# Reading eight retention states over four column groups, with five gate projections moved among them

## The chip, the cores and the metric

One core of a Trainium2 chip runs the whole decoder step as one launch. The metric is device time in microseconds (us) of one launch. Engines are named as in the profile: PE (matrix products) with its weight loads PEld, DVE (vector), ACT (activation), POOL (GpSimd, which here also issues the state transfers) and SP (which issues the weight transfers). Each engine works through its own list in order and meets the others at semaphores.

## The reference, cut to what matters

The step has 256 prompt tokens and a sample group of 8 sequences with one new token each (264 columns in all), a model width of 1024 and everything in float32. The change touches the retention branch of the sample group and the order around it:

```
q, k: 4 heads of 256 (rotary);  v: 4 heads of 512;  g: 2048;  gates g_a, g_b, g_c: 1024 each
for each of 8 sequences b, each of 4 heads h, with s = state_ret[b, h]  (256 x 512):
    s_new = gamma_h * s + k[b,h] (outer) v[b,h]          -> ret_s, an output of 16 MB
    o[b,h] = q[b,h] @ s_new                              (512 numbers)
o = o / sqrt(mean(o*o) + eps) per head
b_out  = (silu(g) * o) @ w_branch_ret
merged = sigmoid(g_a)*a_out + sigmoid(g_b)*b_out + sigmoid(g_c)*c_out ;  x = x + merged @ w_out
then RMSNorm, a mixture of 32 experts over all tokens, residual, final RMSNorm
```

## The kernel before

A Python list, made by `tensor_order()`, holds every task, and each engine walks the same list and does its own part of each task. So a task's place in the list is its place in the queue of PE, ACT and DVE alike; nothing is planned by cost. A projection (`ga`, `lru_out`, `gc`, `mem_out`, `gb`, `g`, ...; lines 988 and 997 in `project`) makes one 128-row tile of output from eight 128x128 weight blocks; each float32 product shows as two instructions in the profile, so it has 16. Projections take turns in PSUM banks 0 to 3, other tasks in banks 4 to 6, and the state reads keep bank 7. Weights come in chunks of two projections (1 MB) into a ring of five places, in list order; SP issues a chunk once the chunk five before it has been used.

**The state stretch.** The 8 x 4 states are handled as 16 steps s of two heads (1 MB each) in three buffers. For each step:

- POOL loads the state (line 895), once that buffer's earlier state is stored and read. It also brings the step's row of v to one partition (line 901) and, when that small transfer has landed, broadcasts it to all partitions (line 905).
- ACT waits for the load and multiplies the state by gamma (task `sd`, two instructions of 128x1024).
- DVE adds the outer product in four instructions of 128x512 (task `sd`, line 1654).
- PE reads the new state against a one-column-per-sequence arrangement of q called `QM` (task `so`, line 1193), and POOL stores it (line 920).

POOL's order is: wait for step s to be updated, store s, bring and broadcast v of s+2, load state s+2. The PE part of `so` for heads 2hp and 2hp+1 writes each head to its own group of 32 PSUM partitions (of 8 used rows):

```
for i in range(2):
    for h2 in range(2):
        h = 2 * hp + h2
        mm = pe.matmul(psum[32 * h:32 * h + NS, 7, :], QM[:, 2 * h + i, b, :], st[:, s % 3, 2 * h2 + i, :], ...)
```

An older task of the same kind, `sc` (line 1132, the sample group's cross-attention), writes four heads to four groups in turn, two products of 256 columns for each head, so 16 instructions in the profile.

**What is woven around it.** The 32 projections `ga`, `lru_out`, `gc`, `mem_out`, woven with the prompt's retention (`att`, four `o`, two `S` per head; lines 1159/1162, 1172/1173, 1181), are the main list, and the 32 items `sd`/`so` are spread evenly over it. In the list, `sd4` stands just before `ga7`, and `att1`, `so3`, `lru_out0`, `o10` follow. `o10` (line 1172) needs DVE's masked copy of `att1` (line 1644), and DVE has `sd4` ahead of it.

**After it.** The eight `gb` projections are woven with `soT` (line 1201: four transposes that bring the 8 tokens' o back to columns), `oq` (squares, ACT, which at the first one waits until all states are stored), and `on` (PE column sums at line 1007, ACT root, DVE lines 1667 and 1669). Then come 16 `g`, 8 `ret_out`, 8 `x2`, the router and the loop over expert pairs.

Of the kernel before, what the change touches and what calls it, by code (L numbers as in the profile page):

```python
# [33 lines left out]
P = 128  # L34
D = 1024
# [27 lines left out]
def shape_constants():  # L63

    f = np.float32
    half = DK // 2
    inv = np.power(f(ROPE_BASE), -np.linspace(0.0, 1.0, half, dtype=f)).astype(f)
    pos = np.concatenate([np.arange(TP), np.full(NS, PAST_LEN)]).astype(f)
    ang = (inv[:, None] * pos[None, :]).astype(f)
    log_g = np.log1p(-(2.0 ** (-5.0 - np.arange(HEADS))))  # L70
    p = np.arange(P)
    mask = np.zeros((P, HEADS, 384))
    for h in range(HEADS):
        n = np.arange(TP)
        mask[:, h, :TP] = np.where(n[None] >= p[:, None], np.exp(np.maximum(n[None] - p[:, None], 0) * log_g[h]), 0)
        mask[:, h, TP:] = mask[:, h, :P]
    kdec = np.zeros((P, 2, HEADS))
    for mt in range(2):
        kdec[:, mt, :] = np.exp((TP - 1 - (mt * P + p))[:, None] * log_g[None])
    valid = np.ones((P, TT))  # L80
    valid[T - 2 * P:, 2] = 0
    parts = {
        "cos": np.cos(ang), "sin": np.sin(ang), "dmask": mask.reshape(P, -1),
        "ident": np.eye(P), "kdec": kdec.reshape(P, -1), "before": (p[:, None] < p[None, :]).astype(f), "valid": valid,
        "slot": np.tile(np.arange(SLOTS), (P, 1)), "count32": np.tile(np.arange(EXPERTS), (P, 1)),
        "count8": np.tile(np.arange(OVER), (P, 1)),
    }
    at, cols, off = {}, [], 0
    for name, a in parts.items():
        at[name] = (off, off + a.shape[1])  # L90
        off += a.shape[1]
        cols.append(a.astype(f))
    return np.ascontiguousarray(np.concatenate(cols, axis=1)), at
# [8 lines left out]

BUFFERS = {
    "rope": (NROPE, "load", "v"),
    "dmask": (NMASK, "load", "gc"),
    "const": (NCONST - NROPE - NMASK, "load", "end"),
    "ones": (P, "load", "end"),
    "chan": (12 * KT, "load", "end"),
# [34 lines left out]
    "uyT": (KT * T, "uy", "ga"),  # L143
    "lru_st": (KT * 16, "ux", "end"),
    "conv_st": (KT * 16, "ux", "end"),
    "qT": (KT * T, "q", "gc"),
    "kT": (KT * T, "k", "gc"),
    "rtmp": (HEADS * 2 * T, "k", "v"),
    "vT": (VT * T, "v", "rows"),
    "v_rows": (2 * HEADS * DV, "rows", "gc"),  # L150
    "k_rows": (2 * D, "v", "gc"),
    "vs_rows": (HEADS * DV, "rows", "gc"),
    "v_row0": (D, "rows", "gc"),
    "vb": (2 * D, "rows", "gc"),
    "st": (3 * 4 * DV, "rows", "gc"),
    "p32": (TP, "k", "k"),
    "PM": (512, "k", "v"),
    "cs": (TP, "k", "rows"),
    "QM": (KT * 64, "k", "gc"),
    "attT": (384, "rows", "gc"),  # L160
    "oT": (VT * T, "ga", "ret"),
    "S_st": (2 * DV, "ga", "gb"),
    "os": (DV, "ga", "gb"),
# [74 lines left out]
def weave(main, side):  # L238

    out, n = [], 0  # L240
    for i, m in enumerate(main):
        out.append(m)
        while n * len(main) < (i + 1) * len(side):
            out.append(side[n])
            n += 1
    return out


def tensor_order():

    t = lambda kind, n: [(kind, i) for i in range(n)]
    heads = range(HEADS)
    lg = [[("lg", h, 0), ("lg", h, 1)] for h in heads]
    pv = [[("pT", h), ("pv", h, 0), ("pv", h, 1)] for h in heads]  # L270
    attn = lg[0] + lg[1] + pv[0] + lg[2] + pv[1] + lg[3] + pv[2] + pv[3]
    gates = [x for n in range(KT) for x in (("r", n), ("i", n))]
    kl = t("kl", NS)
    cache = [("sl",), ("spT",)] + t("sc", NS)
    krows = [("kr", m, q) for m in range(2) for q in range(2)]
    v = t("v", VT)
    vrows = t("vs", 4) + [("vr", m, q) for q in range(4) for m in range(2)]
    ret = []
    for h in heads:
        ret += [("att", h)] + [("o", h, j) for j in range(4)] + [("S", h, i) for i in range(2)]  # L280

    so = [("sd", 0)]
    for s in range(2 * NS):
        so += ([("sd", s + 1)] if s + 1 < 2 * NS else []) + [("so", s)]
    branches = t("ga", 8) + t("lru_out", 8) + t("gc", 8) + t("mem_out", 8)
    onorm = [("soT",), ("oq", 0), ("oq", 1), ("on", 0), ("oq", 2), ("on", 1), ("oq", 3), ("on", 2), ("on", 3)]
    return (

        [("mem_sq",)] + t("mk", 8)[:2] + [("xq",)] + t("mk", 8)[2:4] + [("x_sq",), ("lam",)] + t("mk", 8)[4:]
        + weave(t("mv", 8), t("mkT", 4)) + t("mq", 8) + t("mqs", 2)  # L290

        + weave(t("ux", 8), weave(attn[:11], kl[:2])) + [("conv",)] + weave(t("uy", 8), weave(attn[11:], kl[2:5]))

        + weave(t("q", 8), weave(gates, kl[5:])) + weave(t("k", 8)[:3], cache[:2]) + [("rot_q",)]
        + weave(t("k", 8)[3:], cache[2:5]) + [("rot_k",), ("lru",)]

        + weave(v[:6], cache[5:]) + [("lru_root",), ("gelu",)] + weave(v[6:12], krows) + [("gelu_tanh",)] + v[12:]
        + [("scT",)] + vrows + ret[:1]

        + weave(weave(branches, ret[1:]), so)  # L300

        + weave(t("gb", 8), onorm) + t("g", 16) + t("ret_out", 8) + t("x2", 8) + [("x2_sq",)]
    )


# [27 lines left out]
def build_program(nc, dram, outs, const_at):  # L333
# [55 lines left out]
    with ExitStack() as ctx:  # L389
# [76 lines left out]
        PM = buf("PM").rearrange("p (m h b c) -> p m h b c", m=2, h=HEADS, b=NS)  # L466
        PMd = place_of["PM"]
        cs = buf("cs")
        QM = buf("QM").rearrange("p (k b c) -> p k b c", k=KT, b=NS)
        QMd = place_of["QM"]  # L470
        attT = buf("attT")
        oT = tiles(buf("oT"), VT)
# [38 lines left out]
        def diagonal(at, n):  # L511

            return arena[:, at:at + 64 * n].rearrange("p (k x) -> p k x", x=64)[:, :, 0:64:9]

        psum = ctx.enter_context(nc.psum_tensor("psum", [P, 8, 512], F32))

# [70 lines left out]
        def ps(task):  # L587
            return psum[:, where[task][0], :]
# [372 lines left out]
        def _(pe):  # L961
# [56 lines left out]
            for task in order:  # L1018
# [156 lines left out]
                elif kind == "S":  # L1175
                    _, h, i = task
                    if i == 0:
                        read(pe, ("kr", 1, 1))
                    begin(task)
                    for m in range(2):  # L1180
                        mm = pe.matmul(ps(task)[:, 0:DV], k_rows[:, m, (2 * h + i) * P:(2 * h + i + 1) * P],  # L1181
                                       v_rows[:, m, h * DV:(h + 1) * DV], start=m == 0, stop=m == 1)
                    end(task, mm)
                elif kind == "so":
                    s = task[1]
                    b, hp = n_state(s)
                    if s == 0:
                        pe.wait_ge(bank7_zero, 2)
                    pe.wait_ge(st_updated, s + 1)
                    for i in range(2):  # L1190
                        for h2 in range(2):
                            h = 2 * hp + h2
                            mm = pe.matmul(psum[32 * h:32 * h + NS, 7, :], QM[:, 2 * h + i, b, :],  # L1193
                                           st[:, s % 3, 2 * h2 + i, :],
                                           start=b == 0 and i == 0, stop=b == NS - 1 and i == 1)
                    mm.then_inc(st_read, 1)
                elif kind == "soT":
                    read(pe, ("so", 0))
                    begin(task)
                    for j in range(4):  # L1200
                        mm = pe.transpose(ps(task)[:, j * P:(j + 1) * P], os_[:, j * P:(j + 1) * P], ident)
                    end(task, mm)
                elif kind == "on":
                    pe.wait_ge(squares, 5 + task[1])
                    column_sums(task, sq2[:, task[1] % 2], 4, T)
                elif kind == "x2_sq":
                    residual_squares(KT - 2)
                    end(task, residual_squares(KT - 1))
                else:
                    raise AssertionError(kind)  # L1210
# [266 lines left out]
        def _(dve):  # L1477
# [17 lines left out]
            for task in order:  # L1495
# [100 lines left out]
                elif kind in ("rot_q", "rot_k"):  # L1596
# [3 lines left out]
                    cos, sin = (bc(k_(n).unsqueeze(1), (P, HEADS, T)) for n in ("cos", "sin"))  # L1600
                    read(dve, last["q" if kind == "rot_q" else "k"])

                    full(dve, ("i", KT - 1))
                    v(V.tensor_tensor(t1, x2_, sin, ALU.mult))
                    v(V.tensor_tensor(t2, x1, sin, ALU.mult))
                    v(V.tensor_tensor(x1, x1, cos, ALU.mult))
# [3 lines left out]
                    if kind == "rot_q":  # L1610
                        v(V.memset(QM, 0.0))

                        v(V.tensor_copy(diagonal(QMd, KT), qT[:, :, TP:T]))
                elif kind == "sl":

                    full(dve, ("i", KT - 1))
                    v(V.memset(buf("PM"), 0.0))
                    v(V.memset(psum[:, 7, :], 0.0), bank7_zero)
                    full(dve, task)
# [37 lines left out]
                elif kind == "soT":  # L1657
                    full(dve, task)
                    for h in range(HEADS):
                        did(V.tensor_copy(oT[:, 4 * h:4 * h + 4, TP:T],  # L1660
                                          ps(task).rearrange("p (j c) -> p j c", j=4)[:, :, 32 * h:32 * h + NS]),
                            free_of(task) if h == HEADS - 1 else None)
                elif kind == "on":
                    h = task[1]
# [256 lines left out]
```

## Time and profile before

| | us |
|---|---|
| device time, median of 3 runs | 1262.12 (1260.25 to 1269.47) |
| span of the profiled execution | 1255.6 |
| own device time of the profiled execution | not listed beside its span; the three timed runs are 4.7 to 13.9 above it, their median 6.5 |
| PE busy | 1185.2 (94%) |
| DVE / ACT / POOL busy | 385.5 / 237.3 / 100.3 |
| first to last state read (PE, line 1193) | 333.1 to 500.8 |
| end of the `gb` and norm stage, first `g` | 540.5 |

The span runs from the first to the last instruction of the profiled execution. Times inside the trace count from the start of the span.

### The profile page before, as it was taken

Reading aid. Unit: us, or ns where it says so; the run is one execution under the profiler, and the core shown is the slowest. Engines: PE = TensorE matmul, PEld = TensorE weight load, DVE = VectorE, ACT = ScalarE, POOL = GpSimd, SP = SyncE. Lnnn points to the kernel's source line nnn. Section 1 sums busy time; section 2 is a strip of 40 time slices with the busy share of each in tenths; the row PEclk is TensorE's granted clock in tenths of the full one; section 3 lists DMA queues with packets and bytes.
Section 4 is the critical chain, followed back from the end, with each engine's and each line's share of the span. In section 5 each row is a group of like instructions: output and inputs, shape, how many; then the busy total and the mean of one; then the engine's idle time right before and its main releaser. Section 6 shows DMA issues by size and latency. Waiting matters only on the chain.

```text
span 1255.6 us, 18012 instructions
## 1 busy us (share of the span) xinstructions
PE 1185.2 (94%) x7398; PEld 776.4 (62%) x7398; DVE 385.5 (31%) x696; ACT 237.3 (19%) x449; POOL 100.3 (8%) x127
## 2 busy tenths in 40 slices
PE   6999999999889999999998399999999999999996
PEld 5888888778666766888887154444444444444442
DVE  1203572385323334232111752222211222222222
ACT  2112124123422222321001311111111111111112
POOL 0001120000332322000000400000000000000000
PEclk9999999999999999999999689999999999999999
DMA  8774566675688889335356738999999999999981
GB/s 282 241 256 143 171 210 225 195 244 136 215 273 310 293 279 307 127 126 185 103 167 241 292 135 313 394 394 394 394 394 395 394 394 394 394 394 394 394 310 37
DMA packets 187948, 343.36 MB, mean 273 GB/s; under 512 B 7640, under 2 KB 91864, under 8 KB 187896
## 3 DMA queue, kind: packets, MB, share of 16 engines
q1 hardware_dynamic: 172288, 287.95, 64.2%
q0 software_dynamic: 14464, 52.68, 12.2%
q10 hardware_dynamic: 1152, 2.10, 0.4%
q8 instruction: 33, 0.54, 0.2%
q14 instruction: 11, 0.09, 0.0%
HBM read 320.47 MB, written 22.20 MB: 273 GB/s over the span
## 4 chain that ended last, share of the span: by engine, by line
PE 89%; DVE 6%; ACT 2%; DMA 1%; issue 1%; POOL 0%; DVEq 0%; ACTq 0%
PE psum L988 35%; PE psum L686 18%; PE psum L710 9%; PE psum L648 6%; PE psum L1038 4%; PE psum L723 4%; PE psum L1193 2%; PE psum L997 2%; ACT arena L1240 2%; DVE arena L1808 2%; PE psum L1007 1%; PE psum L1181 1%; DVE arena L1553 1%; DMA arena<-arena 1%; PE psum L1132 1%
## 5 line engine op out<-in xcount | busy, mean ns | idle before, releaser
L988 PE MATMUL psum<-arena 128*128 128x264 f32 x2048 | 473.4, 388 | 0.0
L988 PEld LDWEIGHTS psum<-arena 128*128 128x128 f32 x2048 | 386.1, 190 | 82.2 <-issue 18.6
L1240 ACT ACTIVATE arena<-psum 128x256 f32<-128x256 f32 (+3 forms) x276 | 117.9, 442 | 632.4 <-PE psum L988 263.2
L686 PE MATMUL psum<-arena 128*64 128x512 f32 x1024 | 228.9, 598 | 0.9 <-ACT arena L1240 0.9
L686 PEld LDWEIGHTS psum<-arena 128*64 128x64 f32 x1024 | 73.4, 138 | 141.7 <-issue 141.6
L710 PE MATMUL psum<-arena 128*64 128x512 f32 x512 | 113.4, 595 | 11.1 <-ACT arena L1240 11.1
L1801 DVE SCALAR_TENSOR_TENSOR arena<-arena,psum 128x256 f32<-128x256 f32 x32 | 13.5, 422 | 346.4 <-ACT arena L1240 346.4
L648 PEld LDWEIGHTS psum<-arena 128*128 128x128 bf16 x2304 | 70.7, 99 | 28.0 <-issue 28.0
L1654 DVE SCALAR_TENSOR_TENSOR arena<-arena 128x512 f32<-128x512 f32 x64 | 54.8, 916 | 105.5 <-ACT arena L1240 90.4
L1240 ACT ACTIVATE arena<-arena 128x1024 f32<-128x1024 f32 (+7 forms) x67 | 58.7, 903 | 150.6 <-DVE arena L1694 84.8
L710 PEld LDWEIGHTS psum<-arena 128*64 128x64 f32 x512 | 35.3, 137 | 78.9 <-issue 64.0
L723 PE MATMUL psum<-arena 128*128 128x264 f32 x272 | 78.4, 411 | 5.2 <-ACT arena L1455 1.3
L648 PE MATMUL psum<-arena 128*128 128x64 bf16 x2304 | 74.5, 195 | 2.7 <-DVE arena L1795 2.7
L1808 DVE TENSOR_TENSOR arena<-arena,psum 128x264 f32<-128x264 f32 x136 | 58.3, 429 | 52.5 <-PE psum L723 51.4
L723 PEld LDWEIGHTS psum<-arena 128*128 128x128 f32 x272 | 42.0, 188 | 35.8 <-DVE arena L1808 25.2
L1038 PE MATMUL psum<-arena 128*128 128x256 f32 x256 | 56.3, 379 | 3.1 <-DVE arena L1501 3.1
L1038 PEld LDWEIGHTS psum<-arena 128*128 128x128 f32 x256 | 48.2, 190 | 9.8 <-issue 3.4
L1455 ACT ACTIVATE arena<-psum 128x1024 f32<-128x1024 f32 x16 | 16.4, 1024 | 115.9 <-PE psum L710 115.9
L1193 PE MATMUL psum<-arena 128*8 128x512 f32 x128 | 30.2, 593 | 3.2 <-DVE arena L1654 3.2
L905 POOL PARTITION_BROADCAST arena<-arena x16 | 21.8, 1360 | 106.6 <-DMA arena<-arena 106.6
L997 PE MATMUL psum<-arena 128*128 128x264 f32 x128 | 29.8, 386 | 0.0
L997 PEld LDWEIGHTS psum<-arena 128*128 128x128 f32 x128 | 24.3, 190 | 4.2
(233 smaller groups left out, 641.5 us busy)
## 6 DMA issues: line engine op xcount, KB each, us to landing
arena<-in_w_gate SPq DMA_DIRECT2D x64, 1024.0 KB, 13.5
arena<-in_w_up SPq DMA_DIRECT2D x64, 1024.0 KB, 14.1
arena<-in_w_down SPq DMA_DIRECT2D x64, 1024.0 KB, 12.8
arena<-in_w_in SPq DMA_DIRECT2D x48, 1024.0 KB, 5.3
arena<-in_state_ret POOLq DMA_DIRECT2D x16, 1024.0 KB, 6.8
out_ret_s<-arena POOLq DMA_DIRECT2D x16, 1024.0 KB, 7.6
arena<-in_w_mem_kv SPq DMA_DIRECT2D x8, 1024.0 KB, 9.5
arena<-in_cache_mem_k POOLq DMA_DIRECT2D x8, 1024.0 KB, 5.9
```

The costliest lines, as they stand in the source:

```text
L648: mm = pe.matmul(psum[:, 0, k * SLOTS:(k + 1) * SLOTS], xr[x][:, t, k * P:(k + 1) * P], Sb[:, t, half * SLOTS:(half + 1) * SLOTS], start=t ...
L686: mm = pe.matmul(psum[64 * a:64 * a + SLOTS, 2, :], XgT[:, half, k, :], w[:, :, 256 * a:256 * a + 256], start=k == 0, stop=k == KT - 1)
L710: mm = pe.matmul(psum[64 * half:64 * half + SLOTS, 4 + dh, :], hT[:, half, f % 2, f // 2, :], w[:, f % 2, dh * 512:(dh + 1) * 512], start= ...
L723: pe.matmul(psum[:, 6 + d % 2, 0:T], yS[:, d * P:(d + 1) * P], SwT, start=True, stop=True).then_inc(scatter_full, 1)
L905: nc.gpsimd.partition_broadcast(vb[:, s % 2, :], v_row0[0:1, :], P).then_inc(v_bcast, 1)
L988: mm = pe.matmul(ps(task)[:, 0:T], w[:, k, (i % 2) * P:(i % 2 + 1) * P], rhs[:, k, :], start=k == 0, stop=k == KT - 1 and not two)
L997: mm = pe.matmul(ps(task)[:, 0:T], w[:, k, (i % 2) * P:(i % 2 + 1) * P], rhs[:, KT + k, :], start=False, stop=k == KT - 1)
L1038: mm = pe.matmul(ps(task)[:, 0:256], memT[:, k, m * P:(m + 1) * P], w[:, k, :], start=k == 0, stop=k == KT - 1)
L1193: mm = pe.matmul(psum[32 * h:32 * h + NS, 7, :], QM[:, 2 * h + i, b, :], st[:, s % 3, 2 * h2 + i, :], start=b == 0 and i == 0, stop=b == N ...
L1240: steps.did(nc.scalar.activation(out, in_, func, **kw), sem)
L1654: did(V.scalar_tensor_tensor(x, vb[:, s % 2, h2 * DV:(h2 + 1) * DV], kT[:, 2 * (2 * hp + h2) + i, TP + b:TP + b + 1], x, ALU.mult, ALU.add ...
L1808: V.tensor_tensor(x_res[:, d, :], x_res[:, d, :], psum[:, 6 + d % 2, 0:T], ALU.add).then_inc(scatter_added, 1)
```

## The change

The read of a state uses four column groups, one for each of its four 128-row parts c = 2*h2+i, and both heads' pairs of a step land on 16 rows of each group (`QM` doubles from 64 to 128 columns a tile, zero where nothing belongs). The two halves of a head are then in different groups, so `soT` becomes a product with a constant 0/1 matrix `pairs`, which adds the two halves and brings the result to columns. Five of the eight `gb` projections are appended to the woven main list; the other three stay with `soT`, `oq` and `on`. The lifetimes of eleven buffers are extended to the `gb` stage, so the arena is laid out anew, and three DVE tasks wait for ACT's read of the last LRU gate (`i7`) where they waited for PE's write of it.

```diff
+    pairs = np.zeros((P, HEADS * NS))
+    for h in range(HEADS):
+        for i in range(2):
+            for b in range(NS):
+                pairs[32 * (2 * (h % 2) + i) + NS * (h // 2) + b, NS * h + b] = 1
...
-    "QM": (KT * 64, "k", "gc"),
-    "attT": (384, "rows", "gc"),
+    "QM": (KT * 128, "k", "gb"),
+    "attT": (384, "rows", "gb"),
...
-    branches = t("ga", 8) + t("lru_out", 8) + t("gc", 8) + t("mem_out", 8)
+    branches = t("ga", 8) + t("lru_out", 8) + t("gc", 8) + t("mem_out", 8) + t("gb", 8)[:5]
...
         + weave(weave(branches, ret[1:]), so)
 
-        + weave(t("gb", 8), onorm) + t("g", 16) + t("ret_out", 8) + t("x2", 8) + [("x2_sq",)]
+        + weave(t("gb", 8)[5:], onorm) + t("g", 16) + t("ret_out", 8) + t("x2", 8) + [("x2_sq",)]
...
+        def q_diagonal(hp):
+
+            at = QMd + 512 * hp
+            return arena[:, at:at + 512].rearrange("p (k x) -> p k x", x=128)[:, :, NS * hp:NS * hp + 120:17]
...
-                    for i in range(2):
-                        for h2 in range(2):
-                            h = 2 * hp + h2
-                            mm = pe.matmul(psum[32 * h:32 * h + NS, 7, :], QM[:, 2 * h + i, b, :],
-                                           st[:, s % 3, 2 * h2 + i, :],
-                                           start=b == 0 and i == 0, stop=b == NS - 1 and i == 1)
+                    for c in range(4):
+                        mm = pe.matmul(psum[32 * c:32 * c + 2 * NS, 7, :], QM[:, 4 * hp + c, b, :],
+                                       st[:, s % 3, c, :], start=s == 0, stop=s == 2 * NS - 1)
                     mm.then_inc(st_read, 1)
                 elif kind == "soT":
                     read(pe, ("so", 0))
                     begin(task)
                     for j in range(4):
-                        mm = pe.transpose(ps(task)[:, j * P:(j + 1) * P], os_[:, j * P:(j + 1) * P], ident)
+                        mm = pe.matmul(ps(task)[:, j * 32:(j + 1) * 32], os_[:, j * P:(j + 1) * P], k_("pairs"),
+                                       start=True, stop=True)
                     end(task, mm)
...
-                    full(dve, ("i", KT - 1))
+                    read(dve, ("i", KT - 1))
...
                         v(V.memset(QM, 0.0))
 
-                        v(V.tensor_copy(diagonal(QMd, KT), qT[:, :, TP:T]))
+                        for hp in range(2):
+                            v(V.tensor_copy(q_diagonal(hp), qT[:, 4 * hp:4 * hp + 4, TP:T]))
...
-                                          ps(task).rearrange("p (j c) -> p j c", j=4)[:, :, 32 * h:32 * h + NS]),
+                                          ps(task)[:, 0:P].rearrange("p (j c) -> p j c", j=4)[:, :, NS * h:NS * h + NS]),
```

In the new list one `sd` or `so` follows every second task of the main list. Around the second head's `att` it reads: `ga7 lru_out0 sd4 att1 lru_out1 so3 o10`; at its end: `mem_out7 sd14 o32 gb0 so13 o33 gb1 sd15 gb2 S30 so14 gb3 S31 so15 gb4`, then `gb5 soT oq0 oq1 gb6 on0 oq2 on1 gb7 oq3 on2 on3` and `g`.

## Rows read from the trace of the kernel before

**Rows 1.** Page, chain of work that ended last: shares of the span by engine.
```profile
PE 89%; DVE 6%; ACT 2%; DMA 1%; issue 1%; POOL 0%; DVEq 0%; ACTq 0%
```

**Rows 2.** Stretches (us: length, busy and count of each engine, PE clock, DMA share, GB/s).
```profile
375.92:504.43 128.51, 128.51 (x552) 88.90 (x553) 49.12 (x68) 32.94 (x49) 33.97 (x42) 0.99 0.84 291
504.43:540.47 36.04, 36.04 (x165) 30.79 (x164) 10.53 (x12) 17.44 (x22) 0.00 (x0) 1.00 0.37 120
```

**Rows 3.** Timeline of PE, 326 to 420 (start, us, instruction, idle before and releaser).
```profile
333.14 1.89 PE L1193 MATMUL psum<-arena 128*8 128x512 f32 x8 [3.20 <-DVE arena L1654]
...
368.42 3.83 PE L988 MATMUL psum<-arena 128*128 128x264 f32 x16
375.92 1.22 PE L1172 MATMUL psum<-arena 128*128 128x256 f32 x2 [3.67 <-DVE arena L1644]
...
377.36 4.58 PE L988 MATMUL psum<-arena 128*128 128x264 f32 x16
...
382.53 1.89 PE L1193 MATMUL psum<-arena 128*8 128x512 f32 x8
384.35 3.83 PE L988 MATMUL psum<-arena 128*128 128x264 f32 x16
```

**Rows 4.** Timeline of DVE, 300 to 560.
```profile
371.76 3.64 DVE L1654 SCALAR_TENSOR_TENSOR arena<-arena 128x512 f32<-128x512 f32 x4 [8.57 <-ACT arena L1240]
375.32 0.55 DVE L1644 TENSOR_TENSOR arena<-psum,arena 128x384 f32<-128x384 f32 x1
...
494.37 2.74 DVE L1654 SCALAR_TENSOR_TENSOR arena<-arena 128x512 f32<-128x512 f32 x4 [4.83 <-ACT arena L1240]
```

**Rows 5.** Timeline of ACT, 310 to 550.
```profile
369.65 2.00 ACT L1240 ACTIVATE arena<-arena 128x1024 f32<-128x1024 f32 x2 [7.42 <-DMA arena<-in_state_ret]
```

**Rows 6.** Timeline of POOL, 300 to 520.
```profile
362.62 0.80 POOL L895 DMA_DIRECT2D arena<-in_state_ret  x1
...
409.01 0.76 POOL L920 DMA_DIRECT2D out_ret_s<-arena  x1 [1.94 <-DVE arena L1654]
...
416.29 0.80 POOL L895 DMA_DIRECT2D arena<-in_state_ret  x1
...
431.09 0.75 POOL L920 DMA_DIRECT2D out_ret_s<-arena  x1 [1.40 <-DVE arena L1654]
```

**Rows 7.** Timeline of PE where one state read begins, 343.6 to 343.7.
```profile
343.58 0.60 PE L1193 MATMUL psum<-arena 128*8 128x512 f32 x2
```

**Rows 8.** Timeline of PE where a cross-attention read begins, 257.44 to 257.5.
```profile
257.44 0.40 PE L1132 MATMUL psum<-arena 128*8 128x256 f32 x4
```

**Rows 9.** Timeline of PE, 255 to 300: what follows that read.
```profile
258.42 3.83 PE L988 MATMUL psum<-arena 128*128 128x264 f32 x16
```

**Rows 10.** Timeline of PE, 395 to 560.
```profile
498.95 1.89 PE L1193 MATMUL psum<-arena 128*8 128x512 f32 x8
500.77 7.39 PE L988 MATMUL psum<-arena 128*128 128x264 f32 x32
507.99 0.60 PE L1201 MATMUL psum<-arena 128*128 128x128 f32 x4
508.43 7.29 PE L988 MATMUL psum<-arena 128*128 128x264 f32 x32
...
540.47 19.74 PE L988 MATMUL psum<-arena 128*128 128x264 f32 x88
```

**Rows 11.** Page, costliest groups: instruction, count, busy us, mean ns, idle before.
```profile
L988 PEld LDWEIGHTS psum<-arena 128*128 128x128 f32 x2048 | 386.1, 190 | 82.2 <-issue 18.6
```

**Rows 12.** Stretches, as rows 2: after the wait at `o10`, and before the experts.
```profile
375.90:378.00 2.10, 2.08 (x6) 1.80 (x7) 0.43 (x1) 0.38 (x1) 1.07 (x2) 0.50 0.81 259
...
721.00:730.00 9.00, 7.29 (x80) 4.98 (x82) 8.11 (x28) 0.60 (x1) 0.00 (x0) 0.50 0.01 2
```

**Rows 13.** Timeline of DVE, 195 to 262.
```profile
249.72 1.26 DVE L1604 TENSOR_TENSOR arena<-arena 128x1056 f32<-128x1056 f32 x1 [16.23 <-ACT arena L1240]
```

**Rows 14.** Page, DMA issues: count, KB each, us to landing.
```profile
out_ret_s<-arena POOLq DMA_DIRECT2D x16, 1024.0 KB, 7.6
```

More of the change, by code:

```diff
@@ L85, in shape_constants @@
         "slot": np.tile(np.arange(SLOTS), (P, 1)), "count32": np.tile(np.arange(EXPERTS), (P, 1)),
-        "count8": np.tile(np.arange(OVER), (P, 1)),
+        "count8": np.tile(np.arange(OVER), (P, 1)), "pairs": pairs,
     }
@@ L104 @@
     "rope": (NROPE, "load", "v"),
-    "dmask": (NMASK, "load", "gc"),
+    "dmask": (NMASK, "load", "gb"),
     "const": (NCONST - NROPE - NMASK, "load", "end"),
@@ L145 @@
     "conv_st": (KT * 16, "ux", "end"),
-    "qT": (KT * T, "q", "gc"),
-    "kT": (KT * T, "k", "gc"),
+    "qT": (KT * T, "q", "gb"),
+    "kT": (KT * T, "k", "gb"),
     "rtmp": (HEADS * 2 * T, "k", "v"),
     "vT": (VT * T, "v", "rows"),
[L150 to L155, printed above, removed]
+    "v_rows": (2 * HEADS * DV, "rows", "gb"),
+    "k_rows": (2 * D, "v", "gb"),
+    "vs_rows": (HEADS * DV, "rows", "gb"),
+    "v_row0": (D, "rows", "gb"),
+    "vb": (2 * D, "rows", "gb"),
+    "st": (3 * 4 * DV, "rows", "gb"),
     "p32": (TP, "k", "k"),
@@ L468, in build_program @@
         cs = buf("cs")
-        QM = buf("QM").rearrange("p (k b c) -> p k b c", k=KT, b=NS)
+        QM = buf("QM").rearrange("p (k b c) -> p k b c", k=KT, b=NS, c=2 * NS)
         QMd = place_of["QM"]
@@ L1611, in _ @@
                         v(V.memset(QM, 0.0))
-                        v(V.tensor_copy(diagonal(QMd, KT), qT[:, :, TP:T]))
+                        for hp in range(2):
+                            v(V.tensor_copy(q_diagonal(hp), qT[:, 4 * hp:4 * hp + 4, TP:T]))
                 elif kind == "sl":
-                    full(dve, ("i", KT - 1))
+                    read(dve, ("i", KT - 1))
                     v(V.memset(buf("PM"), 0.0))
```

## The prediction, made before the result was known

> **What bounds it now.** First the chain of waits: PE carries 89% of the time to the end [rows 1], so a microsecond counts only if PE's stream gets shorter or waits less. Next the stretches: from 375.92 to 540.47 PE is busy for the whole length [rows 2], and DMA, at 0.84, has a little room. Third, PE's timeline around the states shows the only two waits of this stage: 3.20 us at the first state read, `so0`, and 3.67 us before `o10` [rows 3]. Fourth, the timelines of DVE, ACT and POOL say who owns the second one. `o10` needs the mask of `att1`, which DVE did at 375.32 to 375.87, straight after it had updated state 4 (371.76 to 375.40) [rows 4]. ACT began the decay of that state at 369.65, when its load landed [rows 5], and POOL had issued that load at 362.62 [rows 6]. No step of that chain waits for PE. So the moment 375.92 is set by the states, and all after it by the length of PE's stream.
>
> The states also have a pace of their own: POOL stores state 7 at 409.01, brings v, issues the load of state 9 at 416.29 and can store state 9 at 431.09 [rows 6], a turn of 22.1 us for two states, 11.0 for one. The last update ends at 494.37 + 2.74 = 497.1 [rows 4]; PE reads it at 498.95 [rows 10], 1.8 us later. So before the change PE and the states finish almost together: a shorter read alone would soon wait for states, and the five projections are what fills that room.
>
> **The price of a read.** A state read takes 384.35 - 382.53 = 1.82 us from its start to the next task's [rows 3]. Its eight instructions start two at a time [rows 7], so there are four rounds. The cross-attention read on four groups starts four at a time [rows 8]: 16 instructions, also four rounds, of half the columns, in 258.42 - 257.44 = 0.98 us [rows 9]. From the two: 512 columns cost (1.82 - 0.98)/4 = 0.21 us a round more than 256, so 0.42 a round, with 0.14 fixed. Eight instructions on four groups are two rounds: 0.84 + 0.14 = 0.98 us; I take a saving of 0.84 to 0.86, 0.85 each. The bounds are 0 (four groups no better than two) and 0.86. By the Trainium skill (TensorE: Matmul & The Clock Gate, Part 3: Packing small matmuls) three column tiles measured 2.38 times the speed of one, not 3; an estimate from it, 3.17 times for four, would put a read at about 1.1 us and the gain of all reads some 1.4 us lower. Rows 8 and 9 show this form without such a loss, so the trace decides.
>
> **The sum, against the profiled execution.** I count from the moment when PE resumes with `o10`.
>
> 1. What comes earlier does not pay. Without the 3.20 us wait (the new list puts one more projection ahead of `so0`, and state 0 is ready at 333.1), with four shorter reads (3.4 us) and one more projection before `o10` (`lru_out1`, 3.61 us, half of 507.99 - 500.77 [rows 10]), PE is at `o10` at about 372.2 - 3.2 - 3.4 + 3.6 = 369.2 rather than at 375.92 - 3.67 = 372.2. DVE still has `sd4` ahead of `att1`. So PE waits until 375.9 again, now some 6.7 us. Gain 0, except:
> 2. `lru_out1` is already done by then: -3.6.
> 3. Twelve reads, `so4` to `so15`, remain after it: 12 x 0.85 = -10.2.
> 4. Five `gb` go from after 504.43 to before: +18 and -18, nothing. Each takes its ACT tanh (free by then, its gate for `mem_out` long passed) and 2.5 chunks of weights along; the order of chunks on SP is the same, and POOL issues nothing for them.
> 5. `soT` becomes eight instructions instead of four, each with a weight load of 190 ns [rows 11]: 1.5 us against 508.43 - 507.99 = 0.44 [rows 10]. I take +1.1; bounds 0 and +1.1, since its moving side is only 32 columns.
> 6. The clock. After the 3.67 us wait PE ran at 0.50 of its clock (1.2 GHz) [rows 12], and the projection at 377.36 took 4.58 us instead of 3.83 [rows 3]; with the half-speed `o10` this cost 1.5. A longer wait may cost more: after the idle time before the experts 0.50 held through 721 to 730 [rows 12], so up to 4.5, 3 more. I take the same 1.5, as the work is the same dense kind, so 0; bounds -1.5 and +3.
> 7. On DVE, `QM`'s clearing doubles and one copy becomes two, behind which DVE is idle for 16.23 us [rows 13]; without that cover it would be under 1 us. The wait for ACT's read of `i7` delays a clearing by about 1 us ahead of idle time. The 16 KB of new constants ride on a 185 KB start transfer. All 0.
>
> Sum: -3.6 - 10.2 + 1.1 = **-12.7 us**. The norm stage then ends at 527.8 instead of 540.5, and what follows is moved as a block. The span becomes 1242.9; what lies around it stays, 6.5 us to the median, so 1262.1 - 12.7 = **1249.4**.
>
> **What covers it.** (a) In this sum PE is at `so15` at 527.8 less `gb4` and the norm stage (3.6 + 3 x 3.6 + 1.5 + 6.8, the last the four `on`: 36.04 us of [rows 2] less eight projections of 3.6 and `soT`) and less the read: 527.8 - 22.7 - 1.0 = 504.1. State 15 is ready at 497.1, a cushion of 7.0 us, though 2.5 MB more on the 37 MB moved there (291 GB/s for 128.5 us [rows 2]) may eat part. (b) Three projections stand between the last read and `on0`, where four stood, and one more up to `on3`, where five more stood. ACT's first `oq` waits for all states to be stored: 497.1 + 0.3 + 7.6 [rows 14] = 505, while PE ends `soT`, which `oq` needs as well, at about 504.1 + 1.0 + 2 x 3.6 + 1.5 = 513.8. So the stores are no wait, with 9 us in hand.
>
> **Rivals.** *The wait at `o10` goes.* If state 4 comes 6.7 us earlier, all 16 reads pay and both waits go: 13.6 + 3.2 + 3.7 + 1.5 - 1.1 = 21 us, 1241. Nothing in the diff touches POOL's turn; a lucky landing gives a part. Chance 0.1.
>
> *Four groups don't overlap* (a read stays 1.82): -3.6 + 1.1, about 1260. Against it [rows 8, 9]. Chance 0.05.
>
> *Slower: the states become the end.* The five `gb` bring weights among state loads and stores. If a turn of 22.1 us grows by x, state 15 is ready 5.5 x later (11 states after state 4); the cushion is gone at x = 1.3, and the stage ends at 540.5 again at x = (7.0 + 12.7)/5.5 = 3.6, 16% longer; for 12.6 us over that x = 5.9. The traffic grows by 2.5 in 37 MB, 7%; if the turn's transfers, some 14 of its 22 us (a load of 7 us, 362.62 to 369.65 [rows 5, 6], and a v row behind a store), grow as much, x = 1.0. So the cushion just holds; a part of the gain may go, and slower takes over three times the estimate: x = 6 gives 1249.4 + 33.0 - 7.0 = 1275. The Trainium skill (Trainium Kernel Development and Optimization, Key Constraints) speaks for this rival: transfers from SP, ACT and POOL share the same 16 engines, so a queue of its own does not protect the states. Chances: 0.1 for a part of the gain lost, 0.05 for slower.
>
> *The norm chain shows* because fewer projections cover it: four root-reciprocal-multiply steps of DVE behind `on0`. PE has four free banks of `g` ahead, 14 us. At worst some 5 us, 1254. Chance 0.05.
>
> **Numbers.** The forecast's own case has 0.65, with items 5 and 6 and the read's price spanning 1247 to 1253. I take 1% of the time, 12.6 us, as what can be told from no change; the forecast sits on that line. Faster by over 1%: 0.36 of the 0.65, all of the first rival: 0.46. Within 1%: 0.29, with 0.05 + 0.1 + 0.05: 0.49. Slower by over 1%: 0.05. The range reaches to the part-lost and the early-state cases: 1243 to 1257.
>
> **What would show it.** Right: line 1193 with about 1.0 us a read and four starts at once; a wait of 6 to 7 us at line 1172 ended by DVE's line 1644 near 375.9; the first `g` near 528. Wrong: a PE wait at line 1193 late in the stretch (states at the end), a wait at line 1007 (norm chain), a read of 1.8 us, or state 4's update well away from 375.4, which would move everything behind it by as much.

## The result

The changed kernel takes 1252.22 us (median of 12 runs, 1247.64 to 1261.76), the kernel before 1261.83 in the runs beside it (12 runs, 1254.28 to 1273.68). The ratio is 0.9935 with a 95% interval of 0.9907 to 0.9963, which is 8 us less (5 to 12). A second set gave 0.9929 (0.9901 to 0.9957). The forecast was 12.7 us. The sign and the range held; a third of the gain is missing. The profiles show waits of PE, and stretches of half clock behind them, in its place.

I call "stage" the stretch of PE's timeline from the start of `ga0` to the start of the first `g`: 540.47 - 321.34 = 219.13 us in the profile before, 539.03 - 324.01 = 215.02 in the first profile after. Lines have moved: 1193 is now 1201 (the read), 1172 is 1182 (`o`), 1654 is 1663 (state update), 1644 is 1653 (mask), 1201 is 1208 (`soT`), 988 is 998.

PE's timeline of the kernel after, 318 to 560:

```profile
336.10 1.05 PE L1201 MATMUL psum<-arena 128*16 128x512 f32 x8
...
380.01 1.22 PE L1182 MATMUL psum<-arena 128*128 128x256 f32 x2 [8.35 <-DVE arena L1653]
...
381.45 5.51 PE L998 MATMUL psum<-arena 128*128 128x264 f32 x16
386.80 0.59 PE L1182 MATMUL psum<-arena 128*128 128x256 f32 x2
...
470.71 3.83 PE L998 MATMUL psum<-arena 128*128 128x264 f32 x16
478.03 1.22 PE L1182 MATMUL psum<-arena 128*128 128x256 f32 x2 [3.49 <-DVE arena L1653]
...
479.47 9.55 PE L998 MATMUL psum<-arena 128*128 128x264 f32 x32
488.95 1.05 PE L1201 MATMUL psum<-arena 128*16 128x512 f32 x8
...
515.69 1.05 PE L1201 MATMUL psum<-arena 128*16 128x512 f32 x8
516.67 7.39 PE L998 MATMUL psum<-arena 128*128 128x264 f32 x32
523.89 0.97 PE L1208 MATMUL psum<-arena 128*128 128x32 f32 x8
524.70 3.81 PE L998 MATMUL psum<-arena 128*128 128x264 f32 x16
...
539.03 21.30 PE L998 MATMUL psum<-arena 128*128 128x264 f32 x95
```

A read takes 516.67 - 515.69 = 0.98 us, where it took 1.82 [rows 3]. The 3.20 us wait at `so0` [rows 3] is gone. The wait at `o10` has grown from 3.67 to 8.35 us, and there is a second of its kind at `o30`, 3.49 us, which the profile before did not have. `soT` takes 524.70 - 523.89 = 0.81 us.

PE's timeline where one read begins; four start together, where it was two [rows 7]:

```profile
345.71 0.62 PE L1201 MATMUL psum<-arena 128*16 128x512 f32 x4
```

DVE's timeline of the kernel after, around both waits (the counterpart of [rows 4]):

```profile
375.85 3.64 DVE L1663 SCALAR_TENSOR_TENSOR arena<-arena 128x512 f32<-128x512 f32 x4 [8.23 <-ACT arena L1248]
379.41 0.54 DVE L1653 TENSOR_TENSOR arena<-psum,arena 128x384 f32<-128x384 f32 x1
...
472.94 3.64 DVE L1663 SCALAR_TENSOR_TENSOR arena<-arena 128x512 f32<-128x512 f32 x4 [6.02 <-ACT arena L1248]
476.50 0.42 DVE L1696 SCALAR_TENSOR_TENSOR arena<-arena,psum 128x264 f32<-128x264 f32 x1
476.95 0.43 DVE L1697 TENSOR_TENSOR arena<-arena 128x264 f32<-128x264 f32 x1
477.42 0.56 DVE L1653 TENSOR_TENSOR arena<-psum,arena 128x384 f32<-128x384 f32 x1
...
507.21 2.74 DVE L1663 SCALAR_TENSOR_TENSOR arena<-arena 128x512 f32<-128x512 f32 x4 [6.68 <-ACT arena L1248]
```

Both masks stand behind a state update: `att1` behind state 4, `att3` behind state 12 and one merge. The last state is ready at 509.95 and read at 515.69, so PE does not meet the states at the end of this profile.

Stretches of the kernel after (columns as in [rows 2]), for the clock behind each wait (the counterpart of [rows 12]):

```profile
380.00:382.50 2.50, 2.49 (x7) 2.10 (x8) 0.42 (x1) 0.38 (x1) 1.06 (x2) 0.50 0.83 236
...
480.00:484.00 4.00, 4.00 (x11) 3.07 (x10) 0.00 (x0) 1.27 (x3) 0.00 (x0) 0.50 0.98 342
484.00:487.00 3.00, 3.00 (x15) 2.58 (x14) 2.03 (x4) 0.83 (x1) 0.11 (x1) 0.99 0.33 112
```

After each wait PE runs at half its clock (0.50, 1.2 GHz) for some 5 to 6 us. Behind the first, 380.01 to 386.80, an `o` with its partner of line 1183 and a projection take 6.79 us, where they take 0.65 + 3.56 at full clock: a loss of 2.6 us. Behind the second, 478.03 to 488.95, it is 10.92 us for 0.65 + 7.22, a loss of 3.0.

### The profile page after: what moved, and what is told of

Same layout as the page of the kernel before. It is cut to its first block, busy times and chain, and to the rows that moved or that the text cites. A ratio compares the mean times of both kernels' runs of the same rounds, so it can differ in the third digit from the quotient of the medians.

```text
span 1250.4 us, 18016 instructions
## 1 busy us (share of the span) xinstructions
PE 1176.1 (94%) x7402; PEld 777.6 (62%) x7402; DVE 384.2 (31%) x697; ACT 232.4 (19%) x445; POOL 101.2 (8%) x127
## 4 chain that ended last, share of the span: by engine, by line
PE 79%; DVE 7%; issue 5%; DMA 4%; ACT 3%; POOL 2%; DVEq 0%; POOLq 0%; ACTq 0%
PE psum L998 28%; PE psum L696 18%; PE psum L720 9%; PE psum L658 6%; PE psum L1048 5%; PE psum L733 4%; ACT arena L1248 2%; DMA arena<-in_state_ret 2%; PE psum L1007 2%; DVE arena L1817 2%; DMA arena<-arena 1%; PE psum L1017 1%; DVE arena L1663 1%; POOL arena L915 1%; DVE arena L1561 1%
## 5 line engine op out<-in xcount | busy, mean ns | idle before, releaser
L1248 ACT ACTIVATE arena<-psum 128x264 f32<-128x264 f32 (+3 forms) x276 | 117.9, 441 | 627.4 <-PE psum L998 252.9
L915 POOL PARTITION_BROADCAST arena<-arena x16 | 22.7, 1416 | 120.8 <-DMA arena<-arena 120.8
L1248 ACT ACTIVATE arena<-psum,arena 128x264 f32<-128x264 f32 (+2 forms) x41 | 19.0, 473 | 33.0 <-DVE arena L1544 22.0
```

The costliest lines, as they stand in the source:

```text
L915: nc.gpsimd.partition_broadcast(vb[:, s % 2, :], v_row0[0:1, :], P).then_inc(v_bcast, 1)
L1248: steps.did(nc.scalar.activation(out, in_, func, **kw), sem)
```

## The experiments

Theory S, written after this result: the waits are set by the states, whose pace is POOL's turn of store, v row and load; PE gets only what it saves beyond them. The first rivals were that PE's stream alone counts (P), that the moved weights slow the states (W), that the waits were chance (N), and that bandwidth paces the states whatever POOL's list says (D).

**after_again**: the changed kernel, no edit.

> The changed kernel once more, to see what one execution differs from the next. Stage = from the start of ga0 to the start of the first g: 219.1 us before, 215.0 in the first profile of the changed kernel, 206.4 by my sum. Theory S (the states' own pace sets when PE resumes at o10 and again at o30): stage 213 to 217 again, waits near 8 us at the mask of att1 and 2 to 4 us at the mask of att3, ratio 0.992 to 0.996. Rival N (the two waits were chance landings of that execution): stage 206 to 211, no wait at att3, ratio near 0.990.

Ratio 0.9929 (0.9901 to 0.9957). PE's timeline has both waits:

```profile
381.07 1.22 PE L1182 MATMUL psum<-arena 128*128 128x256 f32 x2 [9.06 <-DVE arena L1653]
...
475.77 0.70 PE L1182 MATMUL psum<-arena 128*128 128x256 f32 x2 [0.52 <-DVE arena L1653]
```

The stage is 533.82 - 324.37 = 209.45 us. The first wait is there again, as S has it, and the second varies with the execution, as N has it; the ratio is in the range of S, the stage in that of N.

**before_again**: the kernel before, no edit.

> The kernel before once more, one profile: how much states 3 to 15 (133.9 us) and the two waits of PE (3.2 and 3.7 us) differ from one execution to the next. Theory S: the pace was a lucky one and lies between 134 and 142; rival W: again 134 within 1 us.

PE's timeline, 318 to 560:

```profile
336.21 2.66 PE L1193 MATMUL psum<-arena 128*8 128x512 f32 x8 [3.30 <-DVE arena L1654]
...
378.62 0.70 PE L1172 MATMUL psum<-arena 128*128 128x256 f32 x2 [1.65 <-DVE arena L1644]
...
475.26 1.22 PE L1172 MATMUL psum<-arena 128*128 128x256 f32 x2 [8.46 <-DVE arena L1644]
```

The kernel before has the wait at `o30` too, in other executions: 8.46 us here. States 3 to 15 took 142.8 us (updates ending at 364.3 and 507.1), not 133.9 and a little more than S's 142, and the stage 553.04 - 324.32 = 228.72. The profile on which I built was a lucky one: two executions of that kernel differ by ten microseconds in this stage.

**read_only**: the read over four groups, the list as before.

```diff
-    branches = t("ga", 8) + t("lru_out", 8) + t("gc", 8) + t("mem_out", 8) + t("gb", 8)[:5]
+    branches = t("ga", 8) + t("lru_out", 8) + t("gc", 8) + t("mem_out", 8)
-        + weave(t("gb", 8)[5:], onorm) + t("g", 16) + ...
+        + weave(t("gb", 8), onorm) + t("g", 16) + ...
```

> Only the read over four column groups; all eight gb stay behind the states. Theory S: PE is 3.4 us earlier at o10 and waits that much longer, then catches up with the states near the end, so the last read ends 2 to 3 us earlier than before and soT takes 1 us back: ratio 0.997 to 1.001, with waits at the read's line late in the stretch. Rival P (PE's stream alone counts): 16 reads of 0.85 less 1.1, so 12.5 us, ratio 0.990.

Ratio 1.0046 (1.0018 to 1.0074): slower than before, although every read is 0.84 us shorter. Its PE timeline, 318 to 560:

```profile
335.46 1.05 PE L1201 MATMUL psum<-arena 128*16 128x512 f32 x8 [2.97 <-DVE arena L1663]
...
371.25 1.91 PE L1201 MATMUL psum<-arena 128*16 128x512 f32 x8 [4.78 <-DVE arena L1663]
382.99 1.22 PE L1182 MATMUL psum<-arena 128*128 128x256 f32 x2 [5.32 <-DVE arena L1653]
...
466.10 1.26 PE L1201 MATMUL psum<-arena 128*16 128x512 f32 x8 [2.14 <-DVE arena L1663]
...
478.87 1.22 PE L1182 MATMUL psum<-arena 128*128 128x256 f32 x2 [6.32 <-DVE arena L1653]
```

PE outruns the states and waits at both kinds of place, 23 us in all, and after four of the five waits shown its instructions take longer (1.91 and 1.26 for a read, 1.22 for an `o`). P is out. S had the waits, but its 0.997 to 1.001 was missed: it put no price on the clock behind them. In this profile's stage of 553.61 - 323.90 = 229.71 us, PE's work (197.4, see below) and the waits leave some 9 us for half clock. That this is all that S lacked is argued, from one profile.

**gates_only**: the five `gb` moved; read, `QM` and `soT` as before.

```diff
-                    for c in range(4):
-                        mm = pe.matmul(psum[32 * c:32 * c + 2 * NS, 7, :], QM[:, 4 * hp + c, b, :], ...)
+                    for i in range(2):
+                        for h2 in range(2):
+                            h = 2 * hp + h2
+                            mm = pe.matmul(psum[32 * h:32 * h + NS, 7, :], QM[:, 2 * h + i, b, :], ...)
```

> Only the five gb moved among the states; the read stays on two groups and soT stays four transposes. Theory S: the same work in another place, one projection more ahead of the wait at o10, so -3.6 us, and no wait behind it because PE is then well behind the states: ratio 0.996 to 0.999. Rival P: the moved projections change nothing, 1.000. Rival W (the weights moved among the states slow them): state 15 is updated 5 us or more later than before, but PE is later still, so the time stays.

Ratio 0.9958 (0.9934 to 0.9982). Its PE timeline has one wait:

```profile
378.90 1.22 PE L1182 MATMUL psum<-arena 128*128 128x256 f32 x2 [5.87 <-DVE arena L1654]
```

More work among the states means that they are ready when PE comes, even at `o30`. S's 0.996 to 0.999 is just missed by the median and touched by the interval. State 15 is updated 187.6 us after the start of `ga0`, 12 and 5 us later than in the two profiles of the kernel before, and the time does not grow: that is what W expected as well, so this run does not part S from W. The halves are worth -0.4% and +0.5% alone and -0.65% together: with POOL's list as it is, the read pays only where something fills the time that it frees.

**mask_first**: after, with `sd4`, `sd8`, `sd12` just behind their `att`.

```diff
+    for h in range(1, HEADS):
+        at = order.index(("att", h))
+        order.insert(at, order.pop(order.index(("sd", 4 * h))))
...
```

> The changed kernel with sd4, sd8 and sd12 put just behind att1, att2 and att3 in the list, so DVE makes the masks before it updates those states; nothing else. Theory S with the order on DVE as the place: the waits at o10 (8.4 us) and o30 (3.5 us) go, with them the half-speed clock behind each; PE then meets the states late in the stretch, so of some 14 us it keeps 5 to 8: ratio 0.986 to 0.990. Rival Q (the states' pace is all): the waits only move to the read's own line and the ratio stays at that of the changed kernel.

Ratio 0.9871 (0.9837 to 0.9906). Its PE timeline keeps only waits at the read:

```profile
486.63 1.22 PE L1205 MATMUL psum<-arena 128*16 128x512 f32 x8 [2.90 <-DVE arena L1667]
...
508.29 1.91 PE L1205 MATMUL psum<-arena 128*16 128x512 f32 x8 [2.82 <-DVE arena L1667]
```

Five such waits add up to 8.2 us. So the place of the two waits was the order in the list, on DVE above all, and behind it the states' pace is the next limit: 0.6% of the time came back, not all of it. The ratio lies in S's range of 0.986 to 0.990; rival Q of the expectation (the waits only move, the time stays) is right about the place and wrong about the time.

**light_gb**: after, without the weights of the first six `gb`.

```diff
+                if chunk_of[("gb", 0)] <= n <= chunk_of[("gb", 2)]:
+                    sp.dma_start(slot[:, n % RING1, :].rearrange("p (k n) -> p k n", k=KT)[:, 0:1, 0:64],
+                                 chunks[n][:, 0:1, 0:64]).then_inc(chunk_loaded[n % RING1], 16)
+                    continue
```

> The changed kernel with the weights of the first six gb projections (three chunks of 1 MB) not brought, only a corner of each, so those gates come from other weights: no extra weight traffic among the states. Rival W (the moved weights slow the states): states 3 to 15 take 134 us as before instead of 142, state stores land in 7.6 us instead of 9.0, and the time falls by 3 us or more. Theory S without W: state pace within 2 us of the changed kernel's, the time the same.

Ratio 0.9912 (0.988 to 0.9943), which covers the changed kernel's two; it lies 2 to 3 us below them, so the time alone does not exclude W's 3 us. DMA issues between 364 and 510 (count, KB each, us to landing):

```profile
out_ret_s<-arena POOLq DMA_DIRECT2D x13, 1024.0 KB, 9.1
...
arena<-in_w_in SPq DMA_DIRECT2D x3, 32.0 KB, 4.0
```

The three chunks are gone, yet stores land in 9.1 us (9.0 after) and states 3 to 15 take 507.9 - 364.8 = 143.1 us (142.7 after). W is out for the pace of the states. The Trainium skill (Trainium Kernel Development and Optimization, Key Constraints) says that transfers from the SP, ACT and POOL queues run on the same 16 engines; no run contradicts that, but here 38.1 MB instead of 41.0 between 364 and 510 did not show in that pace.

**v_early**: after, with the v row of s+3 fetched right after the broadcast of s+2. `v_fetch` is the part of `v_broadcast` that issues the small transfer; what is left of `v_broadcast` waits for the row and broadcasts it.

```diff
                 if s + 2 < 2 * NS:
                     v_broadcast(s + 2)
+                    if s + 3 < 2 * NS:
+                        v_fetch(s + 3)
                     if s >= 1:
                         load_state(s + 2)
```

> The changed kernel with one edit on POOL's list: the small transfer of the v row of state s+3 is issued right after the broadcast of s+2, so it no longer lies between the store of s and the load of s+2. Theory S (the states' turn sets PE's two waits): POOL's part of a turn falls from about 11 us to about 3.5, state 4 comes some 8 us earlier, the waits at o10 and o30 and the half-speed clock behind them go (11.8 and some 5.5 us in the first profile of the change), the stage shrinks from 215 to about 198, ratio to before 0.978 to 0.983. Rival D (the states are paced by the transfers' bandwidth): the loads only land later, the waits stay above 5 us, ratio 0.990 or more.

1236.4 us, ratio 0.983 (0.9785 to 0.9874). POOL's timeline, one turn:

```profile
416.56 0.75 POOL L934 DMA_DIRECT2D out_ret_s<-arena  x1 [9.33 <-DVE arena L1669]
417.34 1.29 POOL L917 PARTITION_BROADCAST arena<-arena  x1
418.93 0.52 POOL L911 DMA_DIRECT2D arena<-arena  x1 [0.29 <-POOL arena L917]
419.46 0.79 POOL L905 DMA_DIRECT2D arena<-in_state_ret  x1
426.85 0.75 POOL L934 DMA_DIRECT2D out_ret_s<-arena  x1 [6.60 <-DVE arena L1669]
```

From the store to the load of the same turn it is 2.9 us, against 416.29 - 409.01 = 7.3 in [rows 6]; POOL now waits for the states, not they for POOL. What is left of the wait at `o10`, and the end of the stage, in PE's timeline:

```profile
372.76 0.70 PE L1188 MATMUL psum<-arena 128*128 128x256 f32 x2 [0.59 <-DVE arena L1659]
...
522.61 2.61 PE L1004 MATMUL psum<-arena 128*128 128x264 f32 x11
```

Stage 522.61 - 324.53 = 198.08 us, as S expected. D, with waits above 5 us and a ratio of 0.990 or more, is out.

**mask_first_v_early**: both edits.

> Both edits: masks ahead of the state updates on DVE, and the v row fetched early. Theory S: with the turn shortened the order on DVE matters little more, 0 to 2 us below v_early. Rival D: as mask_first, 0.987, since bandwidth still holds the states.

1235.78 us, ratio 0.9825 (0.978 to 0.987), stage 519.53 - 322.10 = 197.43. As S: once the states are in time, DVE's order matters little. v_early, this one and read_only_v_early below are the fastest of all, and by the ratios they can't be told apart.

**before_v_early** and **read_only_v_early**: the same edit of POOL's list on the kernel before, and on read_only.

> The kernel before (read on two groups, all gb behind the states) with the v row fetched early and nothing else. Theory S: its waits at o10 and o30 go too, so what remains is PE's own stream: stage 219.1 less 3.2, 3.7 and 1.5 of the first profile, 210 to 212, against 198.1 of v_early. The difference to v_early is then the whole price of the reads, 16 x 0.84 less about 0.4 for soT: 12 to 14 us. Rival: four groups bring less than their 0.84 a read where PE is never idle, 8 us or less.

> The four-group read with the v row fetched early, all eight gb behind the states. Question: do the moved gb bring anything but cover for late states? Theory S: they are the same work in another place, so with states that keep up the stage is 198 as in v_early, ratio within 0.002 of it. Rival F (filler still needed): PE's stretch among the states is 18 us shorter, 9.4 us a state, which the states' turn does not reach; waits at the read's line appear and the stage is 201 to 208.

Ratios 0.9914 (0.9883 to 0.9945) and 0.9822 (0.9787 to 0.9858). PE's timeline of before_v_early, its one wait and the first `g`:

```profile
332.86 1.89 PE L1199 MATMUL psum<-arena 128*8 128x512 f32 x8 [3.08 <-DVE arena L1660]
...
534.71 10.62 PE L994 MATMUL psum<-arena 128*128 128x264 f32 x47
```

And of read_only_v_early:

```profile
337.06 1.91 PE L1207 MATMUL psum<-arena 128*16 128x512 f32 x8 [3.03 <-DVE arena L1669]
...
527.47 17.74 PE L1004 MATMUL psum<-arena 128*128 128x264 f32 x79
```

Stages: 534.71 - 321.19 = 213.5, a little over the 210 to 212 that took the wait at `so0` as gone (it is still there), and 527.47 - 325.44 = 202.0. With states in time the reads bring 11.5 us of stage, and 0.0092 of the time between the two medians' ratios, against 16 x 0.84 less 0.4 for `soT`, 13.0; the difference is the half clock behind the wait at `so0` in the second (a read of 1.91). Against v_early, the pair that was named beforehand, it is 213.5 - 198.1 = 15.4 us, more than the 12 to 14 expected: v_early has no wait at `so0`, and without that 3.1 us it is 12.3. The moved `gb` bring 202.0 - 198.1 = 4 us of stage, which is that wait of 3.0 and its clock; by ratio the two kernels can't be told apart (0.9822, 0.983). The stage of 202.0 lies in rival F's 201 to 208 and not at S's 198, but F's cause is not there: PE never waits for a state behind `so0`. What S left out is that the moved `gb` cover the wait at `so0`.

PE's own work in the stage can be read from two of these profiles whose clock is 1.00 throughout, before_v_early and mask_first_v_early (columns as in [rows 2], the second number is PE's busy time):

```profile
321.19:534.71 213.52, 210.44 (x927) 152.31 (x926) 66.21 (x102) 65.57 (x95) 51.06 (x60) 1.00 0.74 258
322.10:519.53 197.43, 197.43 (x931) 149.31 (x930) 63.84 (x101) 60.42 (x91) 50.93 (x60) 1.00 0.82 283
```

The change takes 210.4 - 197.4 = 13.0 us of work off PE. What a stage has above that is waits and half clock.

## Why the prediction was right in sign and short in size

1. **The reads**: right. 0.98 us each. The Trainium skill's tile figure (three column tiles 2.38 times; TensorE: Matmul & The Clock Gate, Part 3) would have led to an estimate of some 1.1; the measured read decides against it.
2. **The wait at `o10` swallows what comes earlier** (item 1): right in place and releaser. It was to end near 375.9, which is 54.6 us after the start of `ga0`; it ended at 56.0, and at 56.7 in the second profile: 1.4 to 2.1 us lost. In before_again it was 54.3. The premise that no step of state 4's chain depends on PE is not shown; see the open points.
3. **The clock** (item 6): the term that was mis-sized. I took the old 1.5 us for a wait twice as long; it cost 2.6, some 1.0 more, inside the bound of 3.
4. **No wait behind `o10`**: wrong, and the largest part in the first profile. I had listed only the states' end as the place where late states could show. But `att3` stands behind `sd12` on DVE exactly as `att1` behind `sd4`; the wait there is 3.49 us and 3.0 of clock in one profile, 0.52 in the other. State 15 was taken as ready at 497.1, 175.8 after the start of `ga0`; it came at 185.9 and 185.3, so the cushion of 7.0 us at `so15` was 5.7 in one profile and 0.9 in the other. That the time stayed in the range is in part luck.
5. **`soT`**: 0.37 us over before, not 1.1: its eight weight loads of 192 ns overlap and take 1.08 us together, not 1.5. 0.7 us better than the forecast.
6. **Moved `gb`, norm chain**: right. No wait at the column sums; the stage's tail needed no more cover. The 2.5 chunks of weights did no harm to the states' pace that light_gb could show.
7. **Slower by late states**: not reached in this kernel, and its mechanism (the moved weights slow the states) found no support in light_gb. read_only is slower by late states, 0.5%, but without any moved weights: there PE outruns the states, as the first part of the prediction had warned for a shorter read alone.
8. **What lies around the span**: misread. In every run whose core span is listed, device time is 1.8 to 2.4 us above it. So of the 6.5 us some 4.6 (an estimate) were no margin around the span: the profile was a fast execution of the kernel before.

The sum for the first pair of profiles: reads 12 x 0.84 = -10.1, `lru_out1` -3.7, `soT` +0.4, later resume +1.4, clock +1.0, `o30` +6.5, together -4.5; the stage went from 219.1 to 215.0, -4.1. For the second profile after it is 209.45, -9.7. With PE's own work of 210.4 and 197.4, the waits and their half clock are 8.7 and 18.3 us in the two profiles before, 17.6 and 12.0 in the two after. Single profiles scatter too much to set them against each other; but 13.0 us less work and a timed gain of 8 (5 to 12) leave an estimated 5 us (1 to 8 by that interval) that went, on average, to longer waits and the clock behind them.

What stays open: why state 4 comes 1.4 to 2.1 us later after the change. POOL issues its load at the same moment, 41.3 us after the start of `ga0` before and 41.4 after, but it lands in 8.3 us where it took 7.0 [rows 5, 6]. From the timelines of POOL, ACT and SP of the kernel after, and last SP's of the kernel before:

```profile
365.39 0.80 POOL L905 DMA_DIRECT2D arena<-in_state_ret  x1
373.72 2.00 ACT L1248 ACTIVATE arena<-arena 128x1024 f32<-128x1024 f32 x2 [8.61 <-DMA arena<-in_state_ret]
362.28 38.25 SPq L778 DMA_DIRECT2D arena<-in_w_in  x4
365.39 37.19 SPq L768 DMA_DIRECT2D arena<-in_w_in  x4
```

With POOL's list as it was, this load takes 7.9 to 8.9 us in the five profiles with moved `gb` (light_gb too) and 6.7 to 7.1 in the three without. The weights of `gb` themselves are not sent before 445, but in the new order SP sends a chunk 3.1 us ahead of this load, where it sent one 2.8 us behind it. Whether that chunk is the cause, no run shows: in read_only a chunk goes 4.8 us ahead and the load still takes 6.7.

Open too is how much of the spread of the stage (219 and 229 before, 215 and 209 after) is the chance of landings; two profiles of each can't say. The start of `ga0` also differs, 321.2 to 325.4 over all these profiles, and by 3 us between two of the kernel before (321.34 and 324.32), and so does the time from the first `g` to the end of the span, 711.2 to 715.1 (715.1 and 711.6 in those two); so neither is of the change.

## What to carry to other kernels

A stage in which PE is busy nearly all the time can still be paced by a loop of transfers that finishes just in time: compare the ready time and the use time of each step before shortening PE's side, and look along every queue for work that stands behind that loop (here a mask behind a state update, twice). Where a shorter read and its filler are worth 0.65% together, the cure of the loop itself, one 4 KB transfer issued a turn earlier, was worth another 1%, and 0.9% on the kernel before (0.9914). Price a PE wait with the half-speed microseconds behind it, and take two profiles before building on a wait that is there or not.

## What was not expected of the hardware

A 4 KB transfer took about as long as its neighbours of 1 MB. Issued right behind a store, the v row landed in 7.5 us (median of 16) in the kernel before, where stores took 7.6 [rows 14], and in 8.4 in the changed kernel, where they took 9.0. POOL sat idle for it 120.8 us in all over 16 rows in the changed kernel. In v_early, issued a turn earlier, it landed in 5.5 and left 21.6. From the lists of waits of the two kernels (total us, times, longest):

```profile
POOL arena L915 <- DMA arena<-arena: 120.8, 16, 10.4
POOL arena L917 <- DMA arena<-arena: 21.6, 5, 8.8
```

And the clock does not answer to a wait's length alone. Behind the wait of 3.03 us at `so0` in read_only_v_early the read took 1.91 us instead of 1.05, and behind 3.30 in before_again 2.66 instead of 1.89; behind 3.08 at the same place in before_v_early, and 3.20 in [rows 3], it took its usual 1.89, and behind 2.97 in read_only its usual 1.05. Yet behind 2.14 us late in read_only's stretch the granted clock fell to 0.50.
